# Two-layer-block kernel on one core: the high and low halves of the activations as one 512-column operand

## The reference

```
mixed = (jax.nn.sigmoid(f["g_a"]) * (y_a.astype(dt) @ lp["w_a"])
         + jax.nn.sigmoid(f["g_b"]) * (y_b.astype(dt) @ lp["w_b"]))
return mixed @ lp["w_out"]
...
x = x + gate[:, None] * y.astype(x.dtype)
```

```
h = jnp.matmul(_rmsnorm_2(x, norm_g).astype(x.dtype), w_in).astype(jnp.float32)
...
ya = _dilated_mixture(_rope(_heads(aq, A_HEADS_2), pos), _rope(_heads(ak, A_HEADS_2), pos), _heads(av, A_HEADS_2))
...
yb = _diff_attention(bq[:, :, 0], bq[:, :, 1], bk[:, :, 0], bk[:, :, 1], bv, lam)
...
y = jnp.concatenate([ya, yb], axis=-1) * jax.nn.silu(z)
return x + jnp.matmul(y.astype(x.dtype), w_out)
```

## Time and profile before

| | |
|---|---|
| median of 3 runs | 2584.62 us (2584.35 to 2589.47) |
| the profiled execution | 2587.25 us, of which 2585.4 us are the profile's span |
| TensorE busy | 2458.9 us, 95% of the span, 26124 matmuls |
| TensorE weight loads busy | 2195.3 us, 85% |
| VectorE, ScalarE, GpSimd busy | 1332.2 us (52%), 1162.8 us (45%), 1370.8 us (53%) |
| mean granted TensorE clock | 0.976 |
| chain that ended last | TensorE 85%; L183, L184 and L185 17% each |

### The profile page before, as it was taken

One profiled execution on the slowest core, in us unless ns is written; L12 is line 12 of the kernel. 1 busy time (PEld: TensorE's weight loads), 2 busy tenths in 40 slices (PEclk: granted clock), 3 DMA queues, 4 the chain that ended last, 5 costly groups with the idle time before them and its releaser, 6 DMA issues.

```text
span 2585.4 us, 65221 instructions
## 1 busy us (share of the span) xinstructions
PE 2458.9 (95%) x26124; PEld 2195.3 (85%) x26124; DVE 1332.2 (52%) x2114; ACT 1162.8 (45%) x1712; POOL 1370.8 (53%) x570
## 2 busy tenths in 40 slices
PE   6798999999999799998999999999999999999997
PEld 2276778777877688788999999999999999999997
DVE  5938786767676323335556544544444443333422
ACT  6642443434343233334444455444555554444443
...
GB/s 352 274 109 55 67 45 46 54 67 45 46 54 59 4 82 89 85 86 140 263 241 243 255 180 163 170 163 171 169 156 163 184 166 165 167 171 170 170 172 130
DMA packets 100144, 361.40 MB, mean 140 GB/s; under 512 B 11120, under 2 KB 14320, under 8 KB 99728
## 3 DMA queue, kind: packets, MB, share of 16 engines
...
## 4 chain that ended last, share of the span: by engine, by line
PE 85%; issue 6%; DVE 5%; ACT 2%; DMA 1%; POOL 1%; SPq 0%; DVEq 0%; ACTq 0%; POOLq 0%
PE ps L183 17%; PE ps L184 17%; PE ps L185 17%; PE ps L578 5%; PE ps L579 3%; PE ps L580 3%; PE ps L664 2%; PE ps L730 2%; PE ps L750 1%; PE ps L799 1%; DVE wlo L408 1%; POOL wlo L171 1%; PE ps L767 1%; PE ps L309 1%; DMA W<-stream 1%
## 5 line engine op out<-in xcount | busy, mean ns | idle before, releaser
L171 POOL TENSOR_TENSOR wlo<-raw,whi 128x1024 fp32r<-128x1024 f32 x563 | 1369.6, 2445 | 1192.8 <-ACT whi L161 1055.1
L183 PE MATMUL ps<-ahi,whi 128*128 128x256 f32 (+1 forms) x3712 | 1089.3, 293 | 16.5 <-POOL wlo L171 6.9
L184 PE MATMUL ps<-alo,whi 128*128 128x256 f32 (+1 forms) x3712 | 1074.1, 289 | 0.0
L185 PE MATMUL ps<-ahi,wlo 128*128 128x256 f32 (+1 forms) x3712 | 1073.9, 289 | 0.0
L161 ACT ACTIVATE whi<-raw 128x1024 fp32r<-128x1024 f32 x566 | 595.5, 1057 | 454.0 <-PE ps L185 376.4
L183 PEld LDWEIGHTS ps<-ahi,whi 128*128 128x128 f32 x3712 | 714.7, 193 | 30.6 <-issue 12.5
L184 PEld LDWEIGHTS ps<-alo,whi 128*128 128x128 f32 x3712 | 714.5, 192 | 8.9
L185 PEld LDWEIGHTS ps<-ahi,wlo 128*128 128x128 f32 x3712 | 713.9, 192 | 8.1
L578 PE MATMUL ps<-ahi,whi 128*128 128x256 f32 (+1 forms) x512 | 199.3, 389 | 2.9 <-ACT W L929 2.9
L580 PE MATMUL ps<-ahi,wlo 128*128 128x256 f32 (+1 forms) x512 | 173.3, 338 | 0.8 <-issue 0.8
L579 PE MATMUL ps<-alo,whi 128*128 128x256 f32 (+1 forms) x512 | 173.6, 339 | 0.0
...
## 6 DMA issues: line engine op xcount, KB each, us to landing
...
```

The source lines that it names most:

```text
L171: nc.gpsimd.tensor_tensor(wlo[slot], raw[slot], whi[slot].bitcast(F32), ALU.subtract).then_inc(lo_done, 1)
L183: nc.tensor.matmul(out, whi[slot][:, k, :], mh, start=first and k == 0, stop=False)
L184: nc.tensor.matmul(out, whi[slot][:, k, :], ml, start=False, stop=False)
L185: ins = nc.tensor.matmul(out, wlo[slot][:, k, :], mh, start=False, stop=last and k == UK - 1)
```

## The change

The high and low parts of the activations become one tensor (`acts`, `mhl`), whose first index is the part. In the gates of merge, the three output phases and all heads, `mm_wide` takes the place of `mm_unit`: one matmul of the high weights with high and low activations side by side, 512 columns into a whole bank, and one of the low weights with the high activations, 256 columns into the bank's first half. The sum of the two halves of the bank is made at eviction: ScalarE copies the second half to SBUF (`parts_copy`), VectorE adds it to the first half in PSUM (`parts_sum`), and what read the bank before reads the sum. In the output phases the residual is added in two operations instead. Each product now has a bank of its own: in a head q, k, v and z use banks 0, 1, 2 and 7, query and key are turned and multiplied apart, with the turned half written over the second half of the bank, and `qk` is ready in two steps. The differential heads do the same four times, and use banks 0 to 3 twice. Units 4 and 5 of a merge tile, and all stages before merge, keep three matmuls a slice.

```diff
...
-        ahi = sb("ahi", 2 * KT * T, F32R).ap().rearrange("p (s k t) -> p s k t", s=2, k=KT)
-        alo = sb("alo", 2 * KT * T, F32R).ap().rearrange("p (s k t) -> p s k t", s=2, k=KT)
+        acts = sb("acts", 4 * KT * T, F32R).ap().rearrange("p (b s k t) -> p b s k t", b=2, s=2, k=KT)
+        ahi, alo = acts[:, 0], acts[:, 1]
...
+        def parts_copy(act, held, bank):
+
+            return nc.scalar.activation(held, ps[:, bank, T:], ACT.Copy)
+
+        def parts_sum(dve, held, bank):
+
+            return nc.vector.tensor_tensor(ps[:, bank, 0:T], ps[:, bank, 0:T], held, ALU.add)
+
+        def mm_wide(pe, slot, s, bank, hl, k0, first, last, tile_ready=None):
+
+
+            pe.wait_ge(lo_done, s + 1)
+            both_parts = ps[:, bank, :].rearrange("p (b t) -> p b t", b=2)
             ins = None
             for k in range(UK):
                 if tile_ready is not None:
                     tile_ready(k0 + k)
-                mh, ml = (ahi[:, sel, k0 + k, :], alo[:, sel, k0 + k, :]) if hi_ is None else \
-                    (hi_[:, k0 + k, :], lo_[:, k0 + k, :])
-                nc.tensor.matmul(out, whi[slot][:, k, :], mh, start=first and k == 0, stop=False)
-                nc.tensor.matmul(out, whi[slot][:, k, :], ml, start=False, stop=False)
-                ins = nc.tensor.matmul(out, wlo[slot][:, k, :], mh, start=False, stop=last and k == UK - 1)
+                nc.tensor.matmul(both_parts, whi[slot][:, k, :], hl[:, :, k0 + k, :], start=first and k == 0, stop=False)
+                ins = nc.tensor.matmul(ps[:, bank, 0:T], wlo[slot][:, k, :], hl[:, 0, k0 + k, :], start=False,
+                                       stop=last and k == UK - 1)
...
+        def mm_wide_tile(pe, base, i, per, k, bank, hl):
+
+            mm_wide(pe, (base + k) % RING, i * per + (base + k), bank, hl, 0, True, False)
+            return mm_wide(pe, (base + k + 1) % RING, i * per + (base + k + 1), bank, hl, UK, False, True)
...
-        mhi = mix_stack.enter_context(nc.sbuf_tensor("mhi", [P, KT, T], F32R))
-        mlo = mix_stack.enter_context(nc.sbuf_tensor("mlo", [P, KT, T], F32R))
+        mhl = mix_stack.enter_context(nc.sbuf_tensor("mhl", [P, 2, KT, T], F32R))
+        mhi, mlo = mhl[:, 0], mhl[:, 1]
...
-                    mm_tile(pe, b, i, 12, 0, ps[:, bank, 0:T], 0)
-                    mm_tile(pe, b, i, 12, 2, ps[:, bank + 1, 0:T], 0)
+                    mm_wide_tile(pe, b, i, 12, 0, bank, acts[:, :, 0])
+                    mm_wide_tile(pe, b, i, 12, 2, bank + 1, acts[:, :, 0])
...
+                    parts_copy(act, tg[:, n, 0:T], bank).then_inc(M["gcp"].sem, 1)
+                    M["gsum"].wait(act, i * 4 + 2 * n + 1)
                     nc.scalar.activation(tg[:, n, 0:T], ps[:, bank, 0:T], ACT.Tanh, scale=0.5).then_inc(M["tg"].sem, 1)
                     hi(k + 2, k + 3)
                     act.wait_ge(unit_used, i * 12 + (S_MERGE + k + 4))
+                    parts_copy(act, tg[:, n, T:], bank + 1).then_inc(M["gcp"].sem, 1)
+                    M["gsum"].wait(act, i * 4 + 2 * n + 2)
                     nc.scalar.activation(tg[:, n, T:], ps[:, bank + 1, 0:T], ACT.Tanh, scale=0.5).then_inc(M["tg"].sem, 1)
                     hi(k + 4, k + 5, k + 6)
...
                             M["gate_acc"].wait(dve, (i * 2 + n) * KT + kt)
                             nc.vector.scalar_tensor_tensor(held if kt < KT - 1 else gacc, tile, ck, held, ALU.mult, ALU.add)\
                                 .then_inc(M["gate_acc"].sem, 1)
+                    for g in range(2):
+                        M["gcp"].wait(dve, i * 4 + 2 * n + g + 1)
+                        parts_sum(dve, tg[:, n, T * g:T * g + T], 4 - 4 * n + g).then_inc(M["gsum"].sem, 1)
                     M["tg"].wait(dve, i * 4 + 2 * n + 2)
...
-                            mm_unit(pe, k % RING, i * RING + k, ps[:, bank + n, 0:T], sel, UK * u, u == 0, u == 1, hi_, lo_,
+                            mm_wide(pe, k % RING, i * RING + k, bank + n, hl, UK * u, u == 0, u == 1,
...
-                            nc.vector.tensor_tensor(x, ps[:, bank + n, 0:T], x, ALU.add).then_inc(done.sem, 1)
+                            nc.vector.tensor_tensor(x, ps[:, bank + n, 0:T], x, ALU.add).then_inc(N["half"].sem, 1)
+                            N["half"].wait(dve, i * 2 + n + 1)
+                            nc.vector.tensor_tensor(x, ps[:, bank + n, T:], x, ALU.add).then_inc(done.sem, 1)
...
-                    mm_tile(pe, base, i, U_HEAD, 2, ps[:, 0, T:], 0)
-                    mm_tile(pe, base, i, U_HEAD, 4, ps[:, 1, 0:T], 0)
-                    A["qk"].wait(pe, i + 1)
+                    tile(i, 2, 1)
+                    tile(i, 4, 2)
+                    A["qk"].wait(pe, 2 * i + 2)
                     nc.tensor.matmul(ps[:, 3, 0:P], qk[:, 0:P], qk[:, T:T + P], start=True, stop=True)
                     nc.tensor.matmul(ps[:, 3, P:3 * P], qk[:, P:T], qk[:, T:], start=True, stop=True)\
                         .then_inc(A["s_mm"].sem, 1)
                     A["zz"].wait(pe, i)
-                    mm_tile(pe, base, i, U_HEAD, 6, ps[:, 2, 0:T], 0)
+                    tile(i, 6, 7)
...
-                        A["t1"].wait(pe, i + 1)
-                        unit(i, U_HEAD, ps[:, 0, 0:T], 0)
+                        unit(i, U_HEAD, 0)
...
-                    hi(3)
-                    act.wait_ge(unit_used, i * U_HEAD + (base + 4))
-                    A["t2"].wait(act, i)
-                    for h in range(2):
-                        nc.scalar.activation(rot[64 * h:64 * h + 64, :], ps[64 - 64 * h:128 - 64 * h, 0, :], ACT.Copy)\
-                            .then_inc(A["rot"].sem, 1)
-                    hi(4, 5, 6)
+                    for b in range(2):
+                        act.wait_ge(unit_used, i * U_HEAD + (base + 2 * b + 2))
+                        A["qk"].wait(act, 2 * i)
+                        parts_copy(act, rot[:, T * b:T * b + T], b).then_inc(A["copy"].sem, 1)
+                        A["part"].wait(act, 4 * i + b + 1)
+                        for h in range(2):
+                            nc.scalar.activation(ps[64 * h:64 * h + 64, b, T:], ps[64 - 64 * h:128 - 64 * h, b, 0:T], ACT.Copy)\
+                                .then_inc(A["rot"].sem, 1)
+                        if b == 0:
+                            hi(3)
+                    hi(4, 5)
+                    act.wait_ge(unit_used, i * U_HEAD + (base + 6))
+                    parts_copy(act, vf, 2).then_inc(A["copy"].sem, 1)
+                    hi(6)
...
+                    parts_copy(act, zz, 7).then_inc(A["copy"].sem, 1)
...
-                    A["rot"].wait(dve, 2 * i + 2)
                     A["done"].wait(dve, i)
-                    nc.vector.tensor_tensor(rot, rot, sn, ALU.mult).then_inc(A["t2"].sem, 1)
-                    nc.vector.tensor_tensor(qk, ps[:, 0, :], cs, ALU.mult).then_inc(A["t1"].sem, 1)
-                    A["t1"].wait(dve, i + 1)
-                    A["t2"].wait(dve, i + 1)
-                    nc.vector.tensor_tensor(qk, qk, rot, ALU.add).then_inc(A["qk"].sem, 1)
-                    dve.wait_ge(unit_used, i * U_HEAD + (base + 6))
-                    nc.vector.tensor_tensor(vf, ps[:, 1, 0:T], scale, ALU.mult).then_inc(A["vf"].sem, 1)
+                    for b in range(2):
+                        half = slice(T * b, T * b + T)
+                        A["copy"].wait(dve, 4 * i + b + 1)
+                        parts_sum(dve, rot[:, half], b).then_inc(A["part"].sem, 1)
+                        A["rot"].wait(dve, 4 * i + 2 * b + 2)
+                        nc.vector.tensor_tensor(rot[:, half], ps[:, b, T:], sn[:, half], ALU.mult).then_inc(A["t2"].sem, 1)
+                        nc.vector.tensor_tensor(ps[:, b, 0:T], ps[:, b, 0:T], cs[:, half], ALU.mult).then_inc(A["t1"].sem, 1)
+                        A["t1"].wait(dve, 2 * i + b + 1)
+                        A["t2"].wait(dve, 2 * i + b + 1)
+                        nc.vector.tensor_tensor(qk[:, half], ps[:, b, 0:T], rot[:, half], ALU.add).then_inc(A["qk"].sem, 1)
+                    A["copy"].wait(dve, 4 * i + 3)
+                    parts_sum(dve, vf, 2).then_inc(A["part"].sem, 1)
+                    A["part"].wait(dve, 4 * i + 3)
+                    nc.vector.tensor_tensor(vf, ps[:, 2, 0:T], scale, ALU.mult).then_inc(A["vf"].sem, 1)
...
+                    tile(2)
+                    B["zs"].wait(pe, i)
+                    tile(4)
+                    tile(6)
+                    B["qk"].wait(pe, 4 * i + 1)
+                    tile(8)
+                    B["qk"].wait(pe, 4 * i + 4)
...
+                    turned(0)
                     hi(3)
-                    B["t2"].wait(act, 2 * i)
-                    turned(0)
-                    hi(4, 5, 6, 7)
                     turned(1)
-                    hi(8, 9, 10)
+                    hi(4, 5)
+                    turned(2)
+                    hi(6, 7)
+                    turned(3)
+                    hi(8, 9)
```

(7 more changed lines are left out.)

124 lines of the change are left out of this document (73 added, 51 removed).

## The result

| | before | after |
|---|---|---|
| median | 2586.39 us (2584.35 to 2589.47, 4 runs) | 2623.45 us (2622.82 to 2623.82, 4 runs) |
| the profiled execution | 2587.25 us | 2623.32 us |

The account below looks back on a forecast made before the run. TensorE's own stream was taken to bound the kernel. Stream -36.6, merge +69, differential heads -2 and +4, output phases +1 sum to +35 us on 2587.25, 2622.7; from the 2.6 lower median, forecast 2620 us, range 2596 to 2638.

Parts of the forecast that it names:

- K: In a merge tile, the end of VectorE's 16-operation gate sweep; TensorE was to start unit 5 at K + 4.5 us.
- the walk's two cases: Merge tile period: 20.7 us without a fall of TensorE's clock, L1792's predecessor L1762 held; 21.8 with one, L1762 unhindered.
- the walk: Step-by-step timing of one merge tile from K to the next sweep, at K + 14.5 us, or K + 15.6 with a clock fall.
- the ring: In merge, the cycle of sweep, sum, tanh, split, low half, TensorE, mixing, next sweep; period forecast at 21.6 us, before 17.49.
- the 85 tiles in 100: In merge, the share of tiles taken to have a clock fall and a 21.8 us period, giving 21.6 us on average.
- Rival 2: Merge has the wait but no fall of the clock: period 20.7 us, merge +54 us, 2605 us in all; chance 0.13.
- 347 ns a slice: TensorE's time for one wide and one narrow matmul, for 360 before: 13 ns less, 36.6 us over 352 units outside merge.
- Rival 4: The wide pair takes 360 ns, so the 36.6 us gain falls away: 2656 us; chance 0.10 together with rival 3.
- -9 was said: The three output phases together were predicted to take 9 us less; the second eviction operation was priced at +1 us.
- -4.7: Predicted change of the 4 differential heads in us, including -2 for the L2272 wait and +4 for the value tile.
- rival 3: Softmax weights come 1 us late in each of 28 heads: 28 us more, 2648 us; chance 0.10 together with Rival 4.
- Rival 1: No stall in merge: period 17.07 us, merge -6.7 us, elsewhere -33.6, 2545 us in all; chance 0.10.

Follow-up runs that it names:

- the split's place: Changed kernel with the high halves of the next two units issued before ScalarE's first copy, not behind the first tanh: 2562.53 us, 0.9914 of before.
- the sum's place, The kernel with the sum in the sweep: Changed kernel with VectorE's first gate sum of a merge tile moved behind the fourth of the sweep's 16 operations: 2560.67 us, 0.9899 of before.
- the hold: Changed kernel with the middle results of VectorE's mixing in merge kept in PSUM: 2581.37 us, 0.9981 of before.
- the run with filled idle time: Changed kernel with 16 extra 240-column matmuls ahead of unit 5's in each merge tile: 2622.71 us, 1.0151 of before.

## Why the prediction was right, and where it was not

**Merge, the wait.** Right in each step: the tanh behind the sweep's end, unit 5 at K + 4.5 (4.3), the low halves bunched, GpSimd as releaser. L1788 is held in each of the 16 tiles (2.37 to 2.39 us), and L1792 as the walk's two cases have it: held (1.75 us) in the 7 tiles without a fall of the clock, free (0.42) in the 9 with one, the first tile's among them. The tanh came 1.0 us into the sweep before, not in its middle as the walk has it, which touches no term. Three runs take a different link out of the ring (the split's place, the sum's place, the hold), and each brings the tile from 20.97 to 17.1 or 17.8 us.

**Merge, the size.** Mis-sized. The walk without a fall of the clock gave 20.7, and the run with filled idle time shows 20.4; the falls were to add 0.9 on the mean and added 0.6. Two steps failed. One is the 85 tiles in 100: a fall came in 8 tiles of 15, with idle times of 1.81 to 3.07 us, and none in the others, with 1.39 to 3.05. The other is the price of a fall: these lasted 3.4 us in five tiles and 6.8 in three, 2.5 us a tile, near the 0.85 x 3.2 = 2.7 priced, but part of a fall lies in the idle time and part is given back in the next tile. Together 15 x (21.6 - 20.97) = 9.5 us, and 2 in the first tile. Rival 2, no fall at all, was priced at +54 us for merge; the filled run shows +47.

**The stream.** Mis-sized. 347 ns a slice is right where the fast series holds (merge 346.7), and too low elsewhere: of the third output phase's 256 slices x 13 ns = 3.3 us came 1.7, and 0.4 of them went behind its last unit, so that the phase gained 1.3. The 16 heads, in which both series occur, gave 12.0 of 13.3. The 8 dilated heads gave 4.6 of 6.7 (195.3 us), with the clock at its lower level for 6.8 us at their start; in seven of the other kernels it was there for 3.4 us, as before the change, and they took 194.1 to 194.2. Bounding the pair by 347 and 360 ns was right, taking the lower end in all stages was not. Rival 4 (360 ns everywhere) didn't come.

**Output phases.** -9 was said, -2.1 came. About 4 of the 7 missing us are slices: 350.0, 352.9 and 353.3 ns on the mean in the three phases, and not 347. The second eviction operation was priced at 1 us, in the first phase, and cost 2.5 there, read from start to start: 1.5 in two waits for the eviction of L1889 and 1.0 in five pauses of 0.15 to 0.27 us at later tile pairs. The two waits:

```profile
1548.33 0.50 PE L207 MATMUL ps<-mhl,whi 128*128 128x512 f32 x1 [0.52 <-DVE XR L1889]
...
1560.56 0.50 PE L207 MATMUL ps<-mhl,whi 128*128 128x512 f32 x1 [0.66 <-DVE XR L1889]
```

The kernel with the sum in the sweep has the pauses and neither of the two waits. The three idle times ahead of a norm's sums grew by 0.7 us together. The last 1 us or so isn't accounted for.

**Differential heads.** Wrong in sign in this kernel (+1.1 for -4.7). The wait for L2272 is gone, as said, and the two sums cost TensorE 0.3 us in a head, priced at up to 1; what came on top, in two heads of four, was the second probability operation held by a low half. The rows of before showed this exclusion in merge, and the prediction applied it there and in rival 3, but not to these two operations.

**Heads.** Right: no new wait in 24 heads. Rival 1 (no stall) and rival 3 (heads lose) didn't come; rival 1's period of 17.07 us is, to the digit, what the tile takes once the split or the sum is moved.
